# Expert layers of a two-block transformer kernel: rounding rests for two tiles at a time, whole-row transposes, twelve row sums moved between stages, one Gelu in two pieces

## The reference, cut to what matters

```
def peer_ffn(h, w_q, sub_keys, u_tab, v_tab):
    q = (xc @ w_q).reshape(t, 8, 2, 128)
    sc = einsum('thpc,hpnc->thpn', q, sub_keys)
    v_half, i_half = top_k(sc, 16)
    cand, cand_idx = sums and indices of all 16 x 16 pairs
    top_s, pos = top_k(cand, 16)
    g = softmax(top_s)
    act = gelu(einsum('thkd,td->thk', u_tab[expert], xc))
    return einsum('thk,thkd->td', g * act, v_tab[expert])
```

## Time and profile before

| | |
|---|---|
| median of 3 runs | 2076.83 us (2076.51 to 2081.11) |
| the profiled execution's own time | 2068.39 us |
| its span, first to last instruction | 2066.6 us |
| TensorE products | 2007.3 us, 97% of the span |
| VectorE | 1622.2 us, 78% |
| ScalarE | 857.9 us, 42% |
| GpSimd | 385.0 us, 19% |
| HBM traffic | 511.17 MB, mean 247 GB/s |

### The profile page before, as it was taken

How to read it: one execution, slowest core, us unless ns; L and a number is a source line. 1 busy time by engine, 2 the same in 40 slices (tenths; PEclk the granted TensorE clock), 3 DMA queues, 4 the chain that set the end, 5 groups by cost and what they waited for, 6 DMA issues and landing times.

```text
span 2066.6 us, 35237 instructions
## 1 busy us (share of the span) xinstructions
PE 2007.3 (97%) x12408; PEld 1791.5 (87%) x12408; DVE 1622.2 (78%) x3208; ACT 857.9 (42%) x1653; POOL 385.0 (19%) x262
## 2 busy tenths in 40 slices
PE   8999999999999999999999999999999999999998
PEld 6888887779999999977887887899999998778786
DVE  6899886865799276699999967639964756999997
ACT  6557454545101100055565666531101002555665
POOL 0000000000024233303243100000352322232440
PEclk9999999999999999999999999999999999999999
DMA  6554344415389989867799853335998988678995
GB/s 258 198 203 163 114 139 156 138 67 174 133 337 341 368 321 327 300 241 229 262 351 356 294 184 117 113 117 195 391 353 309 346 306 317 224 243 281 371 377 181
DMA packets 132634, 511.17 MB, mean 247 GB/s; under 512 B 15004, under 2 KB 15132, under 8 KB 129856
## 3 DMA queue, kind: packets, MB, share of 16 engines
q1 hardware_dynamic: 95680, 375.81, 51.7%
q0 software_dynamic: 36864, 134.23, 17.6%
HBM read 508.94 MB, written 1.05 MB: 247 GB/s over the span
## 4 chain that ended last, share of the span: by engine, by line
PE 64%; DVE 16%; DMA 5%; issue 2%; ACT 2%; SPq 0%; DVEq 0%; ACTq 0%
PE bank L2383 30%; PE bank L344 8%; PE bank L346 8%; PE bank L345 8%; DVE tile_lo L2705 5%; DMA wbuf<-in_peer_v 3%; PE bank L2413 3%; PE bank L2414 3%; DVE x_tok L2258 2%; DMA wbuf<-in_peer_u 2%; PE bank L2282 1%; DVE w_parts L2708 1%; DVE e_hot_first L2274 1%; DVE e_hidden L2290 1%; DVE tile_lo L274 1%
## 5 line engine op out<-in xcount | busy, mean ns | idle before, releaser
L2383 PE MATMUL bank<-h_dense,wbuf 128*128 128x192 f32 x4096 | 679.7, 327 | 3.7 <-ACT e_stage L2467 2.4
L2383 PEld LDWEIGHTS bank<-h_dense,wbuf 128*128 128x128 f32 x4096 | 664.2, 190 | 6.0 <-issue 4.9
L2512 ACT ACTIVATE tile_hi<-wbuf 128x1024 fp32r<-128x1024 f32 x248 | 263.0, 1060 | 246.1 <-DMA wbuf<-in_peer_v 202.3
L2705 DVE TENSOR_TENSOR tile_lo<-wbuf,tile_hi 128x1024 fp32r<-128x1024 f32 x256 | 311.0, 1215 | 37.7 <-ACT tile_hi L2512 27.4
L2244 POOL DMA_INDIRECT e_gbuf<-in_peer_v,e_row_at x128 | 227.1, 1774 | 484.3 <-DVE x_tok L2258 445.8
L2494 ACT ACTIVATE e_hidden<-bank 128x384 f32<-128x384 f32 x128 | 62.7, 490 | 603.2 <-PE bank L2383 603.2
L2244 POOL DMA_INDIRECT e_gbuf<-in_peer_rows,e_row_at x128 | 155.8, 1218 | 470.1 <-DVE e_dots L2252 239.0
L2413 PE MATMUL bank<-tile_hi,w_parts 128*128 128x512 f32 x512 | 208.5, 407 | 11.1 <-DVE w_parts L2708 10.4
L274 DVE TENSOR_TENSOR tile_lo<-wbuf,tile_hi 128x1024 fp32r<-128x1024 f32 (+2 forms) x117 | 140.3, 1212 | 80.1 <-ACT tile_hi L266 79.2
L2414 PE MATMUL bank<-tile_lo,w_parts 128*128 128x512 f32 x512 | 200.4, 391 | 0.0
L344 PE MATMUL bank<-tile_hi,w_parts 128*128 128x512 f32 x512 | 200.1, 391 | 0.0
(11 more groups left out here) (391 smaller groups left out, 3500.3 us busy)
## 6 DMA issues: line engine op xcount, KB each, us to landing
wbuf<-in_peer_u SPq DMA_DIRECT2D x256, 512.0 KB, 5.7
wbuf<-in_peer_v SPq DMA_DIRECT2D x256, 512.0 KB, 5.0
wbuf<-in_w_in SPq DMA_DIRECT2D x16, 2048.0 KB, 7.7
wbuf<-in_peer_q SPq DMA_DIRECT2D x32, 512.0 KB, 3.8
wbuf<-in_hyb_in SPq DMA_DIRECT2D x16, 512.0 KB, 3.7
wbuf<-in_mla_uq SPq DMA_DIRECT2D x9, 512.0 KB, 3.4
wbuf<-in_mla_in SPq DMA_DIRECT2D x8, 528.0 KB, 4.2
wbuf<-in_w_v SPq DMA_DIRECT2D x2, 2048.0 KB, 7.3
```

The costliest lines, as they stand in the source:

```text
L2383: last = nc.tensor.matmul(bank[:, j // 2 % 2, j % 2 * S:j % 2 * S + DENSE], ring[:, slot, k * P:(k + 1) * P], h_dense[:, k, :], start=(k = ...
L2512: nc.scalar.activation(tile_hi[:, slot, 0:D], ring[:, slot, 0:D], ACT.Copy).then_inc(hi_done, 1)
L2705: nc.vector.tensor_tensor(tile_lo[:, slot, 0:D], ring[:, slot, 0:D], tile_hi[:, slot, 0:D].bitcast(F32), ALU.subtract).then_inc(lo_done, 1)
```

## The change

Four edits in `expert_layer`, each in effect in both layers:

- ScalarE rounds the activations of two tiles in two copies (2x192 and 2x64 columns) after it has rounded the second of the two V tiles; VectorE takes the rests of both with one subtraction, which stands behind the rest of the first tile; TensorE waits for the pair.
- `dense_turned` transposes all 128 rows of the second tile of tokens (128 columns out), and the next transpose writes over the upper 64 columns.
- `TAKEN` is (16, 30, 36, 90, 92): 90 items are done at the end of the U stage's weighing, 92 at tile 56.
- Gelu of the dots is taken for the first 48 after Gelu pair 44 of the U stage, and for the last 16 after pair 52; the shares are multiplied in by the same pieces.

```
-    TAKEN, LAST_TAKE = (16, 30, 36, 78, 88), 116
-    EXPS_AT, ACTS_AT = (16, 30), 54
+    TAKEN, LAST_TAKE = (16, 30, 36, 90, 92), 116
+    EXPS_AT, ACTS_AT, ACTS = (16, 30), (44, 52), (slice(0, 48), slice(48, SHARED))
...
-            nc.tensor.transpose(out[:, 0:LATE], source(slice(0, LATE), 1), ident[0:LATE, 0:LATE])
-            return nc.tensor.transpose(out[:, LATE:DENSE], source(slice(0, P), 0), ident)
+            nc.tensor.transpose(out[:, 0:P], source(1), ident)
+            return nc.tensor.transpose(out[:, LATE:DENSE], source(0), ident)
...
-            pe.wait_ge(w_lo_done, width * q + base + j + 1)
+            pe.wait_ge(w_lo_done, width // 2 * q + (base + j) // 2 + 1)
...
-        def hidden_rounded(a, slot):
-            part = hidden[:, bass.ds(a, 1), :].rearrange("p a t -> p (a t)")
-            nc.scalar.activation(w_parts[:, slot, LATE + DENSE:LATE + 2 * DENSE], part, ACT.Copy).then_inc(w_hi_done, 1)
-            nc.scalar.activation(w_parts[:, slot, 0:LATE], part[:, 0:LATE], ACT.Copy).then_inc(w_hi_done, 1)
+        def pair_rounded(a, slot):
+            part, slots = hidden[:, bass.ds(a, 2), :], slice(slot, slot + 2)
+            nc.scalar.activation(w_parts[:, slots, LATE + DENSE:LATE + 2 * DENSE], part, ACT.Copy).then_inc(w_hi_done, 1)
+            nc.scalar.activation(w_parts[:, slots, 0:LATE], part[:, :, 0:LATE], ACT.Copy).then_inc(w_hi_done, 1)
...
-            if f == ACTS_AT:
-                act.wait_ge(gather_used, GATHER_0 + SHARED)
-                nc.scalar.activation(acts[:, :], dots[:, :], ACT.Gelu).then_inc(exps_done, 1)
+            if f in ACTS_AT:
+                part = ACTS[ACTS_AT.index(f)]
+                act.wait_ge(gather_used, GATHER_0 + part.stop)
+                nc.scalar.activation(acts[:, part], dots[:, part], ACT.Gelu).then_inc(exps_done, 1)
...
             nc.scalar.activation(tile_hi[:, slot, 0:D], ring[:, slot, 0:D], ACT.Copy).then_inc(hi_done, 1)
-            hidden_rounded(STEP * r + j + SLOTS, j % SLOTS)
+            if j % 2:
+                pair_rounded(STEP * r + j + SLOTS - 1, (j - 1) % SLOTS)
...
-            dve.wait_ge(w_hi_done, 2 * a + 2)
-            hi, lo = (w_parts[:, part, b:b + DENSE] for b in (LATE + DENSE, LATE))
-            nc.vector.tensor_tensor(lo, hidden[:, a, :], hi.bitcast(F32), ALU.subtract).then_inc(w_lo_done, 1)
+            if a % 2 == 0:
+                dve.wait_ge(w_hi_done, a + 2)
+                hi, lo = (w_parts[:, part:part + 2, b:b + DENSE] for b in (LATE + DENSE, LATE))
+                nc.vector.tensor_tensor(lo, hidden[:, a:a + 2, :], hi.bitcast(F32), ALU.subtract).then_inc(w_lo_done, 1)
```

More of the change, by code:

```diff
@@ L2333, in dense_turned @@
         def dense_turned(out, source):
-            nc.tensor.transpose(out[:, 0:LATE], source(slice(0, LATE), 1), ident[0:LATE, 0:LATE])
-            return nc.tensor.transpose(out[:, LATE:DENSE], source(slice(0, P), 0), ident)
+            nc.tensor.transpose(out[:, 0:P], source(1), ident)
+            return nc.tensor.transpose(out[:, LATE:DENSE], source(0), ident)
         def turn_normed(first):
             for k in range(first, first + 4):
-                dense_turned(bank[:, TURN_BANKS[k % 4], 0:DENSE], lambda rows, t: xn[rows, t, k * P:(k + 1) * P]).then_inc(xn_turned, 1)
+                dense_turned(bank[:, TURN_BANKS[k % 4], 0:DENSE], lambda t: xn[:, t, k * P:(k + 1) * P]).then_inc(xn_turned, 1)
         def parts_ready(k):
@@ L2392, in tensor @@
         for j in range(3):
-            dense_turned(bank[:, 2 + j // 2, j % 2 * S:j % 2 * S + DENSE], lambda rows, t: pick[rows, t, j, :]).then_inc(picks_turned, 1)
+            dense_turned(bank[:, 2 + j // 2, j % 2 * S:j % 2 * S + DENSE], lambda t: pick[:, t, j, :]).then_inc(picks_turned, 1)
         with pe.Fori(0, FOURS) as q:
@@ L2491, in scalar @@
                 act.wait_ge(weighted, 2 + NGROUP)
-                for a in range(SLOTS):
-                    hidden_rounded(a, a)
+                for a in range(0, SLOTS, 2):
+                    pair_rounded(a, a)
             nc.scalar.activation(hidden[:, 2 * f:2 * f + 2, :], bank[:, f % 2, :].rearrange("p (a t) -> p a t", t=S)[:, :, 0:DENSE],
@@ L2518, in scalar @@
         for j in range(STEP):
-            if STEP * WEIGHING + j + SLOTS == HALF:
+            if STEP * WEIGHING + j + SLOTS - 1 == HALF:
                 act.wait_ge(weighted, 2 + 2 * NGROUP)
@@ L2649, in take @@
             while taken < min(upto, ITEMS):
+                for n, part in enumerate(ACTS):
+                    if taken == SHARED + part.start:
+                        dve.wait_ge(exps_done, NT + n + 1)
+                        dve.wait_ge(share_done, 2)
+                        nc.vector.tensor_tensor(acts[:, part], acts[:, part], share[:, part], ALU.mult).then_inc(share_done, 1)
+                        dve.wait_ge(share_done, 3 + n)
                 if taken == SHARED:
[L2651 to L2654, removed]
                     dve.wait_ge(rows_zero, 1)
@@ L2731, in vector @@
         nc.vector.tensor_copy(from_low[HIGH, :], x[LOW, 1, :]).then_inc(share_done, 1)
-        dve.wait_ge(share_done, 4)
+        dve.wait_ge(share_done, 5)
         for c in range(2):
```

## The result

The changed kernel takes 2098.1 us (median of six executions; the lowest is 2095.6), the kernel before on the same chips 2083.1 (also six, 2076.5 to 2087.2). One of the six executions after took 11538 us and is left out of the ratio. The ratio is 1.0075, with a 95% interval from 1.0050 to 1.0099: slower by 0.75%, some 15 us, where +2.7 was forecast. The profiled execution after took 2097.36 us, its span 2095.6, at a granted clock of 0.988.

A forecast was written before the change was run, and what follows sets the result against it. V stage bounds: VectorE until tile 56, then the ring's lap; 18.4 us winnable. Terms 1.1 + 0 + 2 - 4.5 + 0.7 + 3.4 = +2.7 us put the median at 2079.5, range 2065 to 2097.

The forecast's parts named there:

- rival A: V stage after tile 56: ScalarE's rounding of the odd tile delays VectorE's pair rest; +14.3 over the sum, 2091 us; chance 0.29.
- After tile 56: V stage, 48 tiles from 56 on: 5.3 us lost in each layer against 5.3 and 1.9 before, so +3.4 us.
- L = 5.3: Landing time in us of V-stage loads after tile 56, expected to fall from a median of 6.7.
- two points of transfers in flight against GB/s: Kernel before: 5.0 in flight at 360 GB/s (V stage), 3.2 at 337 (U stage, layer 0); used to get the landing.
- L + 4.4: Odd slot's lap in us after tile 56: landing plus 4.4, including 0.7 on average for row sums.
- The sign that the forecast named for A: TensorE's tiles from 56 on taking over 119 us.
- Until tile 56: V stage's first 56 tiles: VectorE relieved of row sums, -1.0 us layer 0, -3.5 layer 1; +0.7 separately at tile 0.
- The moved transfers in the U stage: Twelve more row sums and their transfers a layer in the U stage: between nothing and 12.6 us, taken as +2.
- Rival C: U stage: moved transfers fill the memory if only 358 GB/s can be had; +13.3 us, 2090; chance 0.07.
- The transposes: 22 small transposes become whole, 328 ns instead of 271; at most +1.2 us, taken as +1.1.
- Gelu in pieces: U stage: one more ScalarE instruction a layer while it waits for U products; 0 us.
- the likeliest case: The sum as worked out for the whole kernel: +2.7 us, median 2079.5, own range 2073 to 2083; chance 0.36.

The follow-up runs named there:

- after_again: The changed kernel run once more, with no further edit: 2099.4 us, ratio 1.0064 to the kernel before.
- before_eleven: The kernel before with an eleventh product, into a bank nothing reads, for each of tiles 56 to 119: 2105.4 us, a single execution.
- after_sums_left_out: The changed kernel without the last 32 row sums of each layer and their transfers, no gathers beside the loads after tile 56: 2069.5 us.
- before_third: The kernel before, unedited, profiled again later on the chip of `after_again`: 2077.3 us, span 2075.5.
- pairs_only: The kernel before with only the edit that takes activations' rests two tiles at a time: 2103.5 us, ratio 1.0170.
- moved_only: The kernel before with only the twelve row sums moved into the U stage and Gelu in pieces: 2083.5 us, ratio 1.0002.
- before_again: The kernel before, unedited, profiled again on the chip of `pairs_only` and `after_no_pairs`: 2068.8 us.
- after_no_pairs: The changed kernel with activations' rests taken tile by tile, the other edits kept: 2061.2 us, ratio 0.9964.

## Why the prediction was wrong, step by step

The sum's time of 2079.5 was 18.6 us too low, and 2098.1 lies just past the range's upper end of 2097. 6.3 us of the 18.6 are the kernel before itself, 2076.8 in the forecast and 2083.1 beside the result; the change's own miss is 12.3, +15.0 against +2.7. What happened is rival A, whose +14.3 was the right size.

- **The step that failed** is the landing in "After tile 56": L = 5.3, worked out from two points of transfers in flight against GB/s. The lap itself, L + 4.4, was right. By mean the loads of the 48 tiles landed in 6.0 (layer 0) and 6.2 us (layer 1), which makes a lap of 10.4 and 10.6; the mean time from one load to the next into the same slot was 10.4 and 10.6. The forecast's own formula, 48 x (lap / 4 - 2.27) - 3.3, makes of these laps 12.5 and 14.9 us lost; measured are 12.4 and 16.5. Less the 7.2 of before, the term was +3.4 and measured +21.8, with some 2 us behind tile 104. The sign that the forecast named for A, over 119 us in these tiles, is what the trace shows.
- **The landing did not fall.** By median it was 6.3 and 6.8 us after, 6.0 and 6.2 in `after_again`, and 6.1 to 6.7 in the six stretches of the kernel before. The line through the two points does not hold here: the changed kernel moved 318 GB/s at 2.53 us a tile, less than the 337 of the earlier trace rows, and its loads took 6 us all the same, where those of the earlier trace rows took 4.3. The rows of before spoke against that line already: in the same U tiles of layer 1, beside a similar load of gathers, loads took 6.5 (over all loads of the two windows it is 4.1 and 6.1). The forecast counted that for rival A and left it out of the line. And `before_eleven` shows no fall of L with the pace.
- **Why L stays near 6** is only half settled. Without gathers it is 4.3 (`after_sums_left_out`), so in this stage their presence sets it, and `before_eleven` shows that TensorE's pace doesn't. Whether the gathers' share of the 16 DMA engines does it or something else, no run here tells.
- **What the formula can't do.** For the kernel before, with a lap of 9.2, it gives no loss, and 5.3 and 1.9 us were measured there; in `before_third` it was 0.8 and nothing. So it is good to some 5 us a layer, and its close agreement after is in part luck.
- **Until tile 56**: -4.5 and +0.7 forecast, so -3.8. Between tile 0 and tile 56 it was -5.5 against the earlier trace rows and -4.0 against `before_third`, and the step from U to V was 0.7 longer than in `before_third`, for two layers. Right. `pairs_only` (+3.4) and `moved_only` (-5.0 against `before_third`) show that the gain is the moved row sums'.
- **The moved transfers in the U stage**: +2 taken, nothing measured in the stretch where they stand. Tiles 72 to 95 take 69.7 us before and after, although more row sums and gathers run beside them. The row of windows, after, for these tiles of layer 0 (columns as in the earlier trace rows):

```profile
727.30:797.00 69.70, 69.33 (x579) 68.32 (x578) 59.61 (x119) 5.54 (x13) 29.15 (x25) 1.00 0.93 348
```

  against the same tiles before:

```profile
720.10:789.80 69.70, 69.33 (x577) 68.32 (x578) 53.81 (x109) 5.39 (x11) 23.15 (x20) 1.00 0.87 314
```

  Rival C fell: TensorE's pace is the same to 0.1 us. Past tile 72 the U products never waited in the profile after. The transfers asked for less than the forecast's 391 GB/s, 348 in this row. The Trainium skill (DMA: Bandwidth & Descriptors, section Where 436 GB/s comes from) bounds transfers from HBM near 358 GB/s for one core, which it works out as half of a stack's bandwidth. Here one core ran, and `before_third` moved 371 over 110 us, so the trace does not agree.
- **The transposes**: +1.1 forecast, about -5 measured. The forecast allowed a small gain and took a loss; the gain was not small, and no row was looked up for it, though the starts of the transposes stood in the trace before.
- **Gelu in pieces**: 0. No run has it alone; nothing in the U stage's tiles 72 to 127 moved (69.7 and 89.8 us in every trace, to 0.3 us).

Summed over the terms measured against the profile shown of before: -5.5 + 21.8 + 1.9 - 5.0 = +13.2, beside the 15.0 between the medians. Against `before_third` the same sum is -4.0 + 28.3 + 2.1 + 0.7 - 5.0 = +22.1, beside 20.0 between the spans. The size of the loss is known to some 7 us by single profiles; that it lies in the 48 tiles is not in doubt.

What settles the cause: the pairs' edit alone costs more than the whole loss; two statements exchanged on ScalarE, or the pair's rest put behind the odd tile's on VectorE, bring the 48 tiles back to 111 to 113; and where landings are 4.3 and no row sum stands in the lap, the same wait, longer, costs nothing. The forecast's mechanism stands, as its rival A; the likeliest case's own range (2073 to 2083) rested on a landing that no row with gathers in this stage had shown.

## What to carry to other kernels

Before two small operations are merged, ask which of their inputs comes last: the first half now waits for it, and so does all that stands behind it on the engine. In a ring of buffers count the whole lap, from one load's start to the next into the same slot, and place work that doesn't need the arriving tile ahead of the wait for it. A landing time measured with gathers in flight is best carried over unchanged unless a row of the same stage shows it falling.

## What the runs showed of the hardware

**Products of unequal rows follow each other more slowly.** TensorE's timeline of `before_again`, four pairs of transposes of 64 and 128 rows between products:

```profile
493.63 0.28 PE L346 MATMUL bank<-e_q_hi,tile_lo 128*128 128x256 f32 x1
493.84 0.27 PE L2334 MATMUL bank<-cst,e_stage 64*128 64x64 f32 x1
494.04 0.33 PE L2335 MATMUL bank<-cst,e_stage 128*128 128x128 f32 x1
494.30 0.27 PE L2334 MATMUL bank<-cst,e_stage 64*128 64x64 f32 x1
...
495.50 0.36 PE L344 MATMUL bank<-e_q_hi,tile_hi 128*128 128x256 f32 x1
```

and of `after_no_pairs`, where all have 128 rows:

```profile
496.42 0.28 PE L346 MATMUL bank<-e_q_hi,tile_lo 128*128 128x256 f32 x1
496.54 0.27 PE L2334 MATMUL bank<-cst,e_stage 128*128 128x128 f32 x1
496.65 0.27 PE L2335 MATMUL bank<-cst,e_stage 128*128 128x128 f32 x1
496.76 0.27 PE L2334 MATMUL bank<-cst,e_stage 128*128 128x128 f32 x1
...
497.33 0.36 PE L344 MATMUL bank<-e_q_hi,tile_hi 128*128 128x256 f32 x1
```

A pair takes 0.46 us with unequal rows and 0.22 with equal ones, although the durations shown hardly differ: from the first to the second it is 0.20 against 0.11, from the second to the next first 0.26 against 0.11, so each change of the row count costs 0.09 to 0.15 us. A change of columns alone does not: from 256 to 128 columns at 128 rows it is 0.12 (496.42 to 496.54). From the last product ahead of the eight transposes to the first behind them it is 1.87 us against 0.91, so 0.24 a pair and 5.3 over 22 pairs. The forecast compared durations (271 and 328 ns) where the distances between starts decide.

**A landing does not follow the pace.** From 2.27 to 2.6 us a tile, 371 to 318 GB/s, loads of 512 KB beside gathers in the V stage kept landing in 6.0 to 6.8 us by median, and in 4.3 without them at 2.27.
